# Value panels of two attentions as half-height, double-width weight panels

## The reference, cut to what matters

```
k, v = jnp.split(mem_n @ w_xkv, 2, axis=-1)            # w_xkv: 1024 x 2048
q, k, v = jnp.split(h @ w_in, [DIFF_W, 2 * DIFF_W], axis=-1)   # w_in: 1024 x 3072
```

## Time and profile before

| what | value |
|---|---|
| median of three executions | 1373.16 us |
| profiled execution, first to last instruction | 1371.3 us (no other time of its own is given) |
| TensorE busy | 1330.6 us, 97% |
| TensorE weight loads busy | 1272.5 us, 93% |
| VectorE, ScalarE busy | 951.9 us (69%), 657.3 us (48%) |
| granted TensorE clock, mean | 0.991 of full |
| chain of waits that ended last | 80% TensorE, 10% VectorE, 3% DMA, 3% ScalarE |

### The profile page before, as it was taken

One profiled execution on the slowest core, in us unless ns is written; L12 is line 12 of the kernel. 1 busy time (PEld: TensorE's weight loads), 2 busy tenths in 40 slices (PEclk: granted clock), 3 DMA queues, 4 the chain that ended last, 5 costly groups with the idle time before them and its releaser, 6 DMA issues.

```text
span 1371.3 us, 25665 instructions
## 1 busy us (share of the span) xinstructions
PE 1330.6 (97%) x10751; PEld 1272.5 (93%) x10751; DVE 951.9 (69%) x1215; ACT 657.3 (48%) x861; POOL 78.7 (6%) x131
## 2 busy tenths in 40 slices
PE   7999999999999999999999999799999999999998
PEld 7999999988999999999988578799999887999998
DVE  5779886764666777776775868777778866665443
ACT  4544436353533333333556636444446445565442
POOL 4012000000000000011100000000000000000000
PEclk9999999999999999999999999999999999999999
DMA  8665634544288888885551045888984511356551
GB/s 229 202 212 177 191 113 167 163 151 137 89 285 274 270 268 270 274 274 185 153 170 62 1 156 169 284 321 307 319 276 141 189 63 63 124 186 213 184 184 62
DMA packets 172602, 259.11 MB, mean 189 GB/s; under 512 B 5141, under 2 KB 147778, under 8 KB 172514
## 3 DMA queue, kind: packets, MB, share of 16 engines
q1 hardware_dynamic: 160906, 203.13, 45.3%
q0 software_dynamic: 10768, 53.43, 11.2%
q10 hardware_dynamic: 840, 1.28, 0.4%
HBM read 256.77 MB, written 1.05 MB: 188 GB/s over the span
## 4 chain that ended last, share of the span: by engine, by line
PE 80%; DVE 10%; DMA 3%; ACT 3%; issue 2%; SPq 0%; DVEq 0%; ACTq 0%; POOLq 0%
PE ring L693 56%; PE acc L693 22%; DVE w_lo L1984 2%; ACT w_hi L1454 2%; DMA raw<-in_w_mlp_in_dram 2%; DVE arena L2167 1%; DVE arena L2033 1%; ACT arena L1454 1%; PE acc L1250 1%; DMA raw<-in_w_xo_dram 1%; PE ring L1067 1%; DMA raw<-in_w_in_dram 1%; DVE arena L2398 1%; DMA arena<-in_w_ada_dram 0%; ACT h_hi L1454 0%
## 5 line engine op out<-in xcount | busy, mean ns | idle before, releaser
L1984 DVE TENSOR_TENSOR w_lo<-raw,w_hi 128x2048 fp32r<-128x2048 f32 x191 | 436.2, 2288 | 235.7 <-ACT w_hi L1454 235.1
L693 PE MATMUL ring<-h_hi,w_hi 128*128 128x256 f32 (+1 forms) x2016 | 575.6, 286 | 4.8 <-DVE w_lo L1984 1.8
L693 PE MATMUL ring<-h_hi,w_lo 128*128 128x256 f32 (+1 forms) x2016 | 570.0, 283 | 0.0
L693 PE MATMUL ring<-h_lo,w_hi 128*128 128x256 f32 (+1 forms) x2016 | 568.1, 282 | 0.0
L1454 ACT ACTIVATE w_hi<-raw 128x2048 fp32r<-128x2048 f32 x191 | 364.0, 1906 | 235.9 <-DMA raw<-in_w_mlp_out_dram 65.0
L693 PEld LDWEIGHTS ring<-h_hi,w_hi 128*128 128x128 f32 x2016 | 381.6, 189 | 10.4 <-issue 4.4
L693 PEld LDWEIGHTS ring<-h_lo,w_hi 128*128 128x128 f32 x2016 | 382.6, 190 | 2.6 <-issue 2.2
L693 PEld LDWEIGHTS ring<-h_hi,w_lo 128*128 128x128 f32 x2016 | 382.6, 190 | 0.0
L693 PE MATMUL acc<-e_hi,w_hi 128*128 128x256 f32 x768 | 217.6, 283 | 0.5 <-DVE e_lo L2691 0.4
L693 PE MATMUL acc<-e_lo,w_hi 128*128 128x256 f32 x768 | 215.9, 281 | 0.0
L693 PE MATMUL acc<-e_hi,w_lo 128*128 128x256 f32 x768 | 215.9, 281 | 0.0
(11 more groups left out here) (315 smaller groups left out, 1394.9 us busy)
## 6 DMA issues: line engine op xcount, KB each, us to landing
arena<-in_w_ada_dram POOLq DMA_DIRECT2D x64, 768.0 KB, 5.9
raw<-in_w_mlp_in_dram SPq DMA_DIRECT2D x32, 1024.0 KB, 5.5
raw<-in_w_mlp_out_dram SPq DMA_DIRECT2D x32, 1024.0 KB, 5.5
raw<-in_w_in_dram SPq DMA_DIRECT2D x24, 1024.0 KB, 5.2
raw<-in_w_e_gate_dram SPq DMA_DIRECT2D x16, 1024.0 KB, 5.5
raw<-in_w_e_up_dram SPq DMA_DIRECT2D x16, 1024.0 KB, 5.9
raw<-in_w_e_down_dram SPq DMA_DIRECT2D x16, 1024.0 KB, 5.7
raw<-in_diff_w_in_dram SPq DMA_DIRECT2D x12, 1024.0 KB, 5.1
```

What stands on the lines that cost most here:

```text
L693: return nc.tensor.matmul(dst, lhs, rhs, start=start, stop=stop, **kw)
L1984: tt(w_lo[q % SPL][:, 0:n], raw[q % RAW][:, 0:n], w_hi[q % SPL][:, 0:n].bitcast(F32), ALU.subtract)\
```

## The change

The four value panels of each attention become halves: panel (c, kh) holds the input rows kh*512 to kh*512+511 and the columns c*512 to c*512+511, in the order (0,0), (0,1), (1,0), (1,1). A new `wide_rows` takes one such panel and two banks, one for each token tile: for each tile and each of four row blocks it makes three matmuls with 512 moving columns, 24 a panel. The two banks are opened in the first half panel (kh = 0), each just before its first matmul, and are complete only after the second. ScalarE's two copies for a pair therefore both wait for the second panel. In the differential attention ScalarE's program has `ahead(d_v0)` and the root of the head sums before `take_v(0)`.

```diff
+    def halves(w, n0, kh):
+        return w[kh * 512:(kh + 1) * 512, n0:n0 + 512].rearrange("(k p) n -> p k n", p=P)
...
-    add("x_v", [cols(xkv, D + i * HID) for i in range(4)])
+    add("x_v", [halves(xkv, D + c * 512, kh) for c in range(2) for kh in range(2)])
...
-    add("d_v", [cols(d_in, 2 * D + i * HID) for i in range(4)])
+    add("d_v", [halves(d_in, 2 * D + c * 512, kh) for c in range(2) for kh in range(2)])
...
+            def wide_rows(p, kh, fills):
+
+                open_panel(p)
+                wh = w_hi[p % SPL][:].rearrange("p (k n) -> p k n", k=4)
+                wl = w_lo[p % SPL][:].rearrange("p (k n) -> p k n", k=4)
+                for t in range(2):
+                    if kh == 0:
+                        open_fill(fills[t])
+                    o, c = bank(fills[t]), slice(t * P, (t + 1) * P)
+                    for k in range(4):
+                        b = 4 * kh + k
+                        mm(o, h_hi[:, b, c], wh[:, k, :], b == 0, False)
+                        mm(o, h_hi[:, b, c], wl[:, k, :], False, False)
+                        last = mm(o, h_lo[:, b, c], wh[:, k, :], False, b == KB - 1)
+                last.then_inc(S("panel_done"), 1)
...
-                linear_rows(PN["x_v"] + i, x_v_fill(i))
+                wide_rows(PN["x_v"] + i, i % 2, [x_v_fill(i - i % 2 + t) for t in range(2)])
...
-            linear_rows(PN["d_v"], d_v_fill(0))
+            wide_rows(PN["d_v"], 0, (d_v_fill(0), d_v_fill(1)))
             rotate_d(7)
...
-            linear_rows(PN["d_v"] + 1, d_v_fill(1))
+            wide_rows(PN["d_v"] + 1, 1, (d_v_fill(0), d_v_fill(1)))
...
             for i in (2, 3):
-                linear_rows(PN["d_v"] + i, d_v_fill(i))
+                wide_rows(PN["d_v"] + i, i - 2, (d_v_fill(2), d_v_fill(3)))
...
             def take_x_v(i):
-                vals = blk(VALS, 8).rearrange("p (t c) n -> p t (c n)", t=2)[:, :, i * HID:(i + 1) * HID]
+                c, t = divmod(i, 2)
+                vals = blk(VALS, 8).rearrange("p (t c) n -> p t (c n)", t=2)[:, t, c * 512:(c + 1) * 512]
                 ahead(PN["x_v"] + i)
-                act.wait_ge(S("panel_done"), PN["x_v"] + i + 1)
+                act.wait_ge(S("panel_done"), PN["x_v"] + 2 * c + 2)
...
             def take_v(i):
-                vals = blk(D_V, 8).rearrange("p (t c) n -> p t (c n)", t=2)[:, :, i * HID:(i + 1) * HID]
-                if i < 3:
+                c, t = divmod(i, 2)
+                vals = blk(D_V, 8).rearrange("p (t c) n -> p t (c n)", t=2)[:, t, c * 512:(c + 1) * 512]
+                if 0 < i < 3:
                     ahead(PN["d_v"] + i)
-                act.wait_ge(S("panel_done"), PN["d_v"] + i + 1)
+                act.wait_ge(S("panel_done"), PN["d_v"] + 2 * c + 2)
...
-            take_v(0)
+            ahead(PN["d_v"])
             row_root("d_sums", HD)
+            take_v(0)
```

More of the change, by code:

```diff
@@ L1596, in take_x_v @@
             def take_x_v(i):
-                vals = blk(VALS, 8).rearrange("p (t c) n -> p t (c n)", t=2)[:, :, i * HID:(i + 1) * HID]
+                c, t = divmod(i, 2)
+                vals = blk(VALS, 8).rearrange("p (t c) n -> p t (c n)", t=2)[:, t, c * 512:(c + 1) * 512]
                 ahead(PN["x_v"] + i)
-                act.wait_ge(S("panel_done"), PN["x_v"] + i + 1)
+                act.wait_ge(S("panel_done"), PN["x_v"] + 2 * c + 2)
                 f = x_v_fill(i)
-                func(vals, bank(f)[:].rearrange("p (t n) -> p t n", t=2), ACT.Copy).then_inc(S(f"drained{f % BANKS}"), 1)
+                func(vals, bank(f)[:], ACT.Copy).then_inc(S(f"drained{f % BANKS}"), 1)
             act.wait_ge(S("c_done"), 1)
@@ L1915, in take_v @@
             def take_v(i):
-                vals = blk(D_V, 8).rearrange("p (t c) n -> p t (c n)", t=2)[:, :, i * HID:(i + 1) * HID]
-                if i < 3:
+                c, t = divmod(i, 2)
+                vals = blk(D_V, 8).rearrange("p (t c) n -> p t (c n)", t=2)[:, t, c * 512:(c + 1) * 512]
+                if 0 < i < 3:
                     ahead(PN["d_v"] + i)
-                act.wait_ge(S("panel_done"), PN["d_v"] + i + 1)
+                act.wait_ge(S("panel_done"), PN["d_v"] + 2 * c + 2)
                 f = d_v_fill(i)
-                func(vals, bank(f)[:].rearrange("p (t n) -> p t n", t=2), ACT.Copy).then_inc(S(f"drained{f % BANKS}"), 1)
+                func(vals, bank(f)[:], ACT.Copy).then_inc(S(f"drained{f % BANKS}"), 1)
+            ahead(PN["d_v"])
+            row_root("d_sums", HD)
             take_v(0)
-            row_root("d_sums", HD)
             act.wait_ge(S("summed_d_sums"), 1)
```

## The result

The changed kernel is slower. Its median is 1379.57 us (six runs, 1376.50 to 1381.74) against 1373.61 us of the kernel before on the same chip (six runs, 1371.24 to 1374.75). The ratio on record is 1.0050 with an interval of 1.0034 to 1.0065; it is an estimate over all runs and not the quotient of the two medians, which is 1.0043. I had forecast 1375.4 us in a range of 1372.2 to 1378.6. The direction was among my likely ones (0.47 for slower by over 0.2%); the size is outside the range by 1.0 us.

A forecast was written before the change was run, and what follows sets the result against it. TensorE, busy for 97% of the span, was taken as the bound. The memory values' -1.0 us and the differential values' +3.2 (+1.9 +2.3 +0.06 -1.0) gave +2.2 us on the profiled span, so a median of 1375.4 us, range 1372.2 to 1378.6.

The forecast's parts named there:

- The memory values: x_v section: no added wait of TensorE, later copies and splits stay covered, 96 wider matmuls save 1.0 us.
- the cover that I named: c_out1: its split slips to about 217 us, with some 6 us left before TensorE uses it.
- First wait: Middle of d_v0: TensorE waits for VectorE to drain rotation 6's bank behind the split of d_v3, +1.9 us.
- Second wait: Behind d_v1: ScalarE's second take comes after the first take and the copy of d_o0, +2.3 us.
- End: After d_v3: two takes in place of one before the scores of head 1, +0.06 us.
- The sum without the clock: Both attentions: x_v -1.0 and d_v +3.2, together +2.2 us, with no clock fall.
- The clock: Start of d_v2: possible half rate for 3.4 us after the longer low stretch, costing 1.7 us; chance 0.27.
- the likeliest case: The forecast itself: 227 ns per wide matmul, both waits, no clock fall, 1375.4 us; chance 0.35.
- rival 1: Start of d_v2: the clock falls as well, adding 1.7 us, 1377.1 us; chance 0.27.
- No saving per column (2): Wide matmuls in both attentions: 238 ns each, so nothing is gained, +4.1 us, 1377.3 us; chance 0.15.
- Whole overhead gone (3): Wide matmuls in both attentions: 217 ns each, saving 2.0 us a section, +0.4 us, 1373.6 us; chance 0.15.
- Waits covered (4): Differential values: bank drained in time, takes end as before, only savings left, 1371.2 to 1369.3 us; chance 0.08.

The follow-up runs named there:

- both_orders: Changed kernel with ScalarE's copy of d_o0 ahead of take_v(0) and VectorE's rope 6 ahead of the split of d_v3; 1372.33 us, 1.0005 of before.
- early_copy: Changed kernel with ScalarE's copy of d_o0 moved ahead of take_v(0); 1376.90 us, 1.0026 of the kernel before.
- filler3: Changed kernel with three keep_busy calls between the two groups of spreads behind d_v1; 1375.91 us, 1.0025 of the kernel before.
- d_only: Changed kernel with the memory values (x_v) restored, wide panels for the differential values alone; 1378.82 us, 1.0053 of the kernel before.
- rope_first: Changed kernel with only VectorE's order altered, rope 6 ahead of the split of d_v3; 1376.64 us, 1.0041 of the kernel before.
- full_again: The changed kernel itself, unaltered, run once more on another run's chip; 1379.15 us, 1.0062 of the kernel before.
- x_only: Changed kernel with the differential values (d_v) restored, wide panels for the memory values alone; 1372.93 us, 1.0006 of the kernel before.
- filler: Changed kernel with eight keep_busy calls between the two groups of spreads behind d_v1; 1378.13 us, 1.0034 of the kernel before.
- full: The change as it is, against the kernel before; 1379.57 us (1.0050) at first, 1379.15 us (1.0062) when repeated.

## Why the prediction was wrong in size, point by point

The profiles give TensorE's time from the end of the last key panel (d_k3) to the end of d_v3, panel by panel, from the timeline of each kernel (us):

| kernel | to the end of d_v0 | d_v1 | d_v2 | d_v3 | together | half rate behind d_v1 |
|---|---|---|---|---|---|---|
| before | 7.41 | 8.63 | 8.72 | 5.69 | 30.45 | none |
| both_orders | 7.26 | 8.49 | 9.01 | 5.58 | 30.34 | none |
| early_copy | 9.13 | 8.49 | 9.02 | 5.58 | 32.22 | none |
| filler3 | 9.13 | 8.49 | 10.81 | 5.58 | 34.01 | none |
| d_only | 9.13 | 8.49 | 12.38 | 5.57 | 35.57 | 3.4 us |
| rope_first | 7.26 | 8.49 | 13.52 | 5.58 | 34.85 | 6.8 us |
| after | 9.13 | 8.49 | 13.57 | 5.57 | 36.76 | 6.8 us |

The end of a panel is the start of its last matmul plus one distance, 0.12 us at 256 columns and 0.23 at 512. For d_k3 in the kernel after that is 1087.22 us:

```profile
1087.10 0.28 PE L696 MATMUL ring<-h_hi,w_lo 128*128 128x256 f32 x1
```

- **The memory values: right, but the saving was forecast at almost twice what came.** No new wait, the copy of c_out0 at 208.60 us (forecast 208.5) and the split of c_out1 at 216.19 (forecast about 217), under the cover that I named. The saving is 0.57 us in place of 1.04, because the distance is 232 ns and not 227: 96 x (237.8 - 231.9) = 0.57.
- **First wait: right.** Forecast +1.9 us; in the timeline 1.76 for the gap and 0.11 for the slower start behind it. The column is 1.72 longer, which is that less the panel's share of the saving, 0.15.
- **Second wait: right.** filler3 shows it without the clock: d_v2 starts 5.19 us behind the end of d_v1 in place of 2.95, which is 2.24 more where I had 2.3. The column grows by 2.09, with the panel's shorter stream.
- **End: +0.1 us** from the end of d_v3 to the first panel behind the heads (40.82 us in place of 40.72), where I put 0.06.
- **The sum without the clock** by the profiles: x_v -0.6, the four columns 34.01 - 30.45 = +3.56, the end +0.1, together +3.1 us. The forecast was +2.2. The 0.9 us between them are one mis-sized term, the distance, in two sections: 2 x 0.47.
- **The clock: the step that failed.** I left it out of the likeliest case (chance 0.27) and priced it at 1.7 us. In the columns it is 12.38 - 10.81 = 1.6 us where it lasted 3.4 us, as priced, and 13.57 - 10.81 = 2.8 us where it lasted 6.8, which I left out although held a fall of that length. All four profiles that kept the late copy and filled nothing show a fall behind d_v1 (after, d_only, full_again, rope_first); none of before, x_only, early_copy, filler, filler3 and both_orders does. The earlier trace rows had the fall behind a stretch with 2.67 of 4.50 us busy; mine was to be 5.25 us long with only the two spread groups in it, 1.7 us, so it lay beyond a known case of falling. That reading would have made rival 1 the likelier forecast, though not a sure one, since the same stretch doesn't always bring a fall. Behind the stretch of the earlier trace rows at 22 us the clock fell in seven of the eleven profiles; in x_only, with the same work, it did not:

```profile
22.00:26.50 4.50, 2.66 (x23) 1.00 0.57 174
26.60:30.00 3.40, 3.40 (x31) 1.00 0.88 279
```

And the kernel before has a fall for which no pause answers:

```profile
730.00:736.50 6.50, 6.50 (x58) 1.00 0.38 125
736.50:743.40 6.90, 6.90 (x37) 0.51 0.23 81
```

So the runs show that the fall behind d_v1 goes with the second wait left unfilled, and not by what rule the clock falls. The Trainium skill says that pauses bring back the half clock ("TensorE: Matmul & The Clock Gate", "Why this matters for your kernels"), and the runs agree with it behind d_v1: 2.46 of 5.20 us busy, with pauses of 2.0 and 0.8 us, was followed by 0.50, and 3.90 of 5.20 by 1.00. It doesn't explain the fall at 736.5 us.

How the terms add up over all runs, not only in the profiles, can be seen by the granted clock that each run lists. Time lost to a low clock is about (1 - clock) x 1371 us; what is left is waits and work. This is an upper estimate, since half rate costs less where TensorE idles anyway. (Among the executions of one kernel the time changes by about 0.76 us for each 0.001 of the clock, and not by 1.37.) The mean of before is over 66 executions, its clock over the 60 that list one; its mean on one chip or another is 1371.9 to 1373.7 us.

| kernel (runs) | mean us | clock | against before | of it clock | the rest |
|---|---|---|---|---|---|
| before (66) | 1372.5 | 0.9920 | | | |
| full, both times (12) | 1379.6 | 0.9896 | +7.1 | +3.3 | +3.8 |
| x_only (12) | 1373.0 | 0.9916 | +0.5 | +0.6 | -0.1 |
| d_only (6) | 1379.1 | 0.9900 | +6.6 | +2.8 | +3.9 |
| rope_first (7) | 1377.4 | 0.9890 | +5.0 | +4.1 | +0.8 |
| early_copy (12) | 1375.9 | 0.9909 | +3.4 | +1.5 | +1.9 |
| filler (11) | 1377.6 | 0.9920 | +5.1 | 0.0 | +5.1 |
| filler3 (9) | 1375.9 | 0.9918 | +3.4 | +0.3 | +3.1 |
| both_orders (12) | 1372.7 | 0.9912 | +0.2 | +1.1 | -0.8 |

The last column is uncertain by some 0.5 to 0.8 us (one standard error of the runs' scatter, with the clock taken out), and by up to 1 us for the chips. Within that, +3.8 for full agrees with the +3.1 of the profiles, and filler3 with +3.1. The clock accounts for a quarter to a half of the loss: 1.6 to 2.8 us in the columns, 2.2 to 3.3 by filler3, of 6 to 7. The columns' clock and the +3.1 us together give 4.7 to 5.9, so up to 2 us stay unexplained. Part of each kernel's clock term is chance: in every kernel the clock also falls at other places (near 302, 364, 736 and 887 us in these profiles), and which of these falls a run has differs from run to run.

**The range** left out rivals 1 and 2 together, at 1379.0 us. What came is nearly that: the clock fell, and the saving was 0.57 us a section where I took 1.04. The two have nothing to do with each other, so they should not have stood as cases that exclude one another, and rival 1 should have carried the price of the longer fall.

**Rivals.** No saving per column (2): the distance of 232 ns lies halfway between my 227 and its 238, and the sum without the clock, +3.1 us, between my +2.2 and its +4.1. Whole overhead gone (3): excluded by 232 ns. The formula of the Trainium skill ("TensorE: Matmul & The Clock Gate", "Back-to-back issue gap") for isolated matmuls, 216 ns at 512 columns, is off by 16 ns for fp32r here. Waits covered (4): excluded by the two waits in the profile. With the two edits of both_orders they are gone but for 0.45 us, and even then the kernel only ties with before.

**Open.** Why fp32r matmuls stand 119 ns apart at 256 columns and 232 at 512, where the columns at 2.4 GHz are 107 and 213, is not settled. That the 112 ns at 128 columns are the stationary load was expected and is not shown; the earlier trace rows have 118 ns with 48 stationary columns at 256 moving ones, which speaks against the load as the cause at that width. Why a fall lasts 3.4 us in one profile and 6.8 in another was not tried, and neither was how often it comes in each kernel, since only the profiled executions show the place.

## What to carry to other kernels

When a product is made wider so that two tiles accumulate over two panels, ask two things of the in-order engines around it: which bank now opens earlier, and what its drain stands behind; and which two evictions now come at the same moment, and what stands between them. Here both answers were a weight split of about 2 us that could as well be done elsewhere, and moving two calls took back all 0.5%. Price a new wait of TensorE with the half-clock stretch that may follow it: if the trace shows a fall behind a denser stretch than the one you are making, count the fall in the likeliest case. And measure the distance at the width you go to: halving the number of matmuls gave 6 ns a pair.

## What the runs showed of the hardware that I had not expected

- In fp32r with 128 stationary columns the distance between matmuls was 112 ns at 128 moving columns, 119 at 256 and 232 at 512 (at 1.2 GHz 0.43 us for 512). 128 columns were nearly as dear as 256.
- A `keep_busy` call in fp32 at 256 columns occupied TensorE for 0.43 us in two records of 0.22 us each.
- More work on TensorE made the kernel faster. With three filling calls (1.56 us of matmuls that nobody reads) d_v2 ran at a granted clock of 1.00 where it had begun at 0.50, and the loss against before was 3.8 us in place of 6.0 to 7.1.
- The half-rate stretch behind the same code lasted 3.4 us in some profiles and 6.8 in others, and at 26.6 us it came in seven profiles of eleven. Two runs of one kernel differ by more than such a fall costs (1368.59 to 1376.52 us for before on one chip).
